# Down projections of six feed-forward stages moved into seven-product units, interleaved with the gate and up units

## What is computed

```
def swiglu(x, w_gate, w_up, w_down):
    return (jax.nn.silu(x @ w_gate) * (x @ w_up)) @ w_down
```

## Time and profile before

| | us |
|---|---|
| median of 3 runs | 3017.22 (3016.87 to 3020.1) |
| the profiled execution, its time | 3015.58 |
| its span in the profile | 3014.3 |
| PE busy | 2961.4 |
| DVE busy | 1835.2 |
| ACT busy | 1348.4 |
| POOL busy | 583.4 |

### The profile page before, as it was taken

One profiled execution on the slowest core, in us unless ns is written; L12 is line 12 of the kernel. 1 busy time (PEld: TensorE's weight loads), 2 busy tenths in 40 slices (PEclk: granted clock), 3 DMA queues, 4 the chain that ended last, 5 costly groups with the idle time before them and its releaser, 6 DMA issues.

```text
span 3014.3 us, 46624 instructions
## 1 busy us (share of the span) xinstructions
PE 2961.4 (98%) x19086; PEld 2616.7 (87%) x19086; DVE 1835.2 (61%) x2832; ACT 1348.4 (45%) x2332; POOL 583.4 (19%) x495
## 2 busy tenths in 40 slices
PE   9999999999999999999999999999999899999999
PEld 7998877899988999886789988899998768788888
DVE  6884566688746887365598853744323866554432
ACT  5552376455524554266455532522223556542321
POOL 0222143302221123034311131100003222200000
PEclk9999999999999999999999999999999999999999
DMA  4333331133332233332223333233233111133332
GB/s 138 113 101 114 97 98 57 57 96 102 115 103 83 92 106 120 93 112 63 64 71 99 106 118 93 78 91 87 90 89 116 50 35 42 36 105 97 93 90 78
DMA packets 76533, 270.10 MB, mean 90 GB/s; under 512 B 8720, under 2 KB 9008, under 8 KB 76064
## 3 DMA queue, kind: packets, MB, share of 16 engines
q1 hardware_dynamic: 74448, 260.08, 28.4%
q0 software_dynamic: 1872, 7.04, 0.7%
HBM read 264.97 MB, written 2.11 MB: 89 GB/s over the span
## 4 chain that ended last, share of the span: by engine, by line
PE 88%; DVE 8%; ACT 2%; issue 1%; DMA 0%; SPq 0%; POOL 0%; DVEq 0%; ACTq 0%
PE psum L424 17%; PE psum L427 17%; PE psum L430 17%; PE psum L677 8%; PE psum L682 8%; PE psum L680 7%; PE psum L488 4%; PE psum L500 2%; PE psum L447 1%; PE psum L443 1%; PE psum L1208 1%; PE psum L445 1%; PE psum L3356 1%; DVE z_sum L1365 1%; DVE w_lo L811 0%
## 5 line engine op out<-in xcount | busy, mean ns | idle before, releaser
L377 DVE TENSOR_TENSOR w_lo<-w_raw,w_hi 128x1024 fp32r<-128x1024 f32 (+1 forms) x300 | 397.2, 1330 | 646.8 <-ACT w_hi L366 646.7
L366 ACT CAST w_hi<-w_raw 128x1024 fp32r<-128x1024 f32 (+1 forms) x346 | 351.4, 1019 | 685.4 <-PE psum L430 643.2
L424 PE MATMUL psum<-x_hi,w_hi 128*128 128x512 f32 (+1 forms) x1648 | 511.2, 351 | 2.6 <-ACT neg_mean L3427 1.8
L427 PE MATMUL psum<-x_hi,w_lo 128*128 128x512 f32 (+1 forms) x1648 | 493.2, 340 | 0.9 <-DVE w_lo L377 0.9
L430 PE MATMUL psum<-x_lo,w_hi 128*128 128x512 f32 (+1 forms) x1648 | 491.2, 339 | 0.1
L424 PEld LDWEIGHTS psum<-x_hi,w_hi 128*128 128x128 f32 x1648 | 283.1, 188 | 58.4 <-issue 18.4
L427 PEld LDWEIGHTS psum<-x_hi,w_lo 128*128 128x128 f32 x1648 | 282.8, 188 | 37.8 <-issue 4.8
L430 PEld LDWEIGHTS psum<-x_lo,w_hi 128*128 128x128 f32 x1648 | 282.8, 189 | 35.9 <-DVE x_lo L3865 0.8
L424 PE MATMUL psum<-h_hi_ffn,w_hi 128*128 128x512 f32 (+1 forms) x792 | 296.4, 374 | 0.0
L430 PE MATMUL psum<-h_lo_ffn,w_hi 128*128 128x512 f32 (+1 forms) x792 | 292.6, 369 | 0.0
L427 PE MATMUL psum<-h_hi_ffn,w_lo 128*128 128x512 f32 (+1 forms) x792 | 292.6, 369 | 0.0
(11 more groups left out here) (436 smaller groups left out, 6760.2 us busy)
## 6 DMA issues: line engine op xcount, KB each, us to landing
w_raw<-in_ffn_gu SPq DMA_DIRECT2D x176, 512.0 KB, 3.6
w_raw<-in_ffn_down SPq DMA_DIRECT2D x64, 512.0 KB, 3.6
w_raw<-in_w_in SPq DMA_DIRECT2D x44, 512.0 KB, 3.6
w_raw<-in_b_gate SPq DMA_DIRECT2D x44, 512.0 KB, 3.6
w_raw<-in_b_up SPq DMA_DIRECT2D x44, 512.0 KB, 3.6
w_raw<-in_b_down SPq DMA_DIRECT2D x32, 512.0 KB, 3.5
w_raw<-in_ffn_down SPq DMA_DIRECT2D x32, 384.0 KB, 3.2
w_raw<-in_b_in SPq DMA_DIRECT2D x24, 512.0 KB, 3.6
```

The costliest lines, as they stand in the source:

```text
L366: nc.scalar.copy(w_hi[s][:, 0:n], w_raw[r][:, 0:n]).then_inc(*w_high.inc(u))
L377: nc.vector.tensor_tensor(w_lo[s][:, 0:n], w_raw[r][:, 0:n], w_hi[s][:, 0:n].bitcast(F32), ALU.subtract).then_inc(*w_low_dve.inc(u))
L424: nc.tensor.matmul(out, w_h, hi[:, c], start=first and i == 0, stop=False)
L427: nc.tensor.matmul(out, w_l, hi[:, c], start=False, stop=False)
```

## The change

- All six FFNs use the combined form, the two of the second block too, with four direct hidden tiles each.
- The first 18 of the 22 contraction tiles of the down projections are taken in three chunks of six (`CHUNKS`). A unit `("d", c, j)` multiplies a chunk with outputs 2j and 2j+1 in seven products of 3 contraction tiles (9 matmuls each); a chunk has four such units. `ffn_units` gives the order: a chunk's units stand among the gate and up units (`"g"`) of the next chunk. A stage has 18 `g` units and 12 `d` units.
- The last four contraction tiles (`TAIL`) are done in direct form at the end, in token halves (16 products of 12 matmuls of 256 columns), with the norm in the manner of `MixNorm` (class `FfnEnd`; `FfnNorm` now derives from `MixNorm`).
- Hidden tiles (class `Hidden`) are held as turned pairs for the first nine pairs (`TURNED`). POOL makes them: `n1`, `t3`, `n2`, `t4` of 256 columns (L630), low parts (L641), and a low part of 4x256 columns (L648) behind one more cast on ACT (`act_turn`). `dve_hidden_low` is gone from DVE.
- A `d` unit adds to `x` in place: POOL first adds each copy `r`, `p1`, `p2` to `x` (`pool_add`, L1199, L1201), then DVE joins (L1114, L1142).
- In `b2_ffn1` POOL applies the late root in the combined form, three more instructions for each hidden tile (`pool_root`).

The core of the diff:

```diff
-COMBINED = {"ffn1_0": 4, "ffn2_0": 4, "ffn1_1": 4, "ffn2_1": 4}
+FIRST_TILES = 4
+COMBINED = {"ffn1_0": 4, "ffn2_0": 4, "ffn1_1": 4, "ffn2_1": 4, "b2_ffn1": 4, "b2_ffn2": 4}
+CHUNKS = ((0, 6), (6, 6), (12, 6))
+TAIL = 18
+TURNED = TAIL // 2
...
+def ffn_units(f0):
+
+    grown = lambda first, end: [("g", f) for f in range(first, end)]
+    down = lambda c, *js: [("d", c, j) for j in js]
+    return (grown(f0, 8) + down(0, 0, 1) + grown(8, 9) + down(0, 2) + grown(9, 10) + down(0, 3)
+            + grown(10, 14) + down(1, 0, 1) + grown(14, 15) + down(1, 2) + grown(15, 16) + down(1, 3)
+            + grown(16, 20) + down(2, 0) + grown(20, 21) + down(2, 1) + grown(21, FT) + down(2, 2, 3))
...
+            def pool_step(self, f):
+
+                for made in self.ready[f]:
+                    pool.wait_ge(*made)
+                if f // 2 < TURNED:
+                    for name in ("t3", "n2", "t4") if f % 2 else ("n1",):
+                        self.pool_combine(name, f // 2)
+                pool.wait_ge(*self.high.at(("h", f)))
+                c, hi, lo = self.of(f)
+                nc.gpsimd.tensor_tensor(lo, self.tile(f)[:, c], hi.bitcast(F32),
+                                        ALU.subtract).then_inc(*self.low.inc(("h", f)))
+
+            def pool_turn(self, pair):
+
+                pool.wait_ge(*self.high.at(("turn", pair)))
+                hi, lo = self.blocks(pair, 3, 4)
+                nc.gpsimd.tensor_tensor(lo, self.raw[:], hi.bitcast(F32),
+                                        ALU.subtract).then_inc(*self.low.inc(("turn", pair)))
...
+                if self.down(i):
+                    even, odd = self.targets(i)
+                    out = {"gate_a": even[:, self.a], "gate_b": even[:, self.b],
+                           "up_b": odd[:, self.b]}[name]
+                    dve.wait_ge(*self.added.at((part, i)))
+                    nc.vector.scalar_tensor_tensor(
+                        out, self.out(b), -self.scale if name == "up_b" else self.scale, snap,
+                        ALU.mult, ALU.add).then_inc(*self.joined.inc((name, i)))
+                    return
...
+            def pool_root(self, name, i):
+
+                tile = self.h.tile(self.units[i][1])
+                c = {"a": self.a, "b": self.b, "again": self.h.columns}[name]
+                if name == "again":
+                    pool.wait_ge(*self.silu.at(self.units[i][1]))
+                else:
+                    pool.wait_ge(*self.joined.at(("gate_" + name, i)))
+                nc.gpsimd.tensor_tensor(tile[:, c], tile[:, c], z_sum[:, c], ALU.mult).then_inc(
+                    *self.rooted.inc((name, i)))
...
+            def pool(self, total):
...
+                for i in range(n + 1):
+                    if i and self.down(i - 1):
+                        self.pool_add("p2", i - 1)
+                    elif i and late:
+                        self.pool_root("b", i - 1)
+                    if i < n and self.down(i):
+                        self.pool_add("r", i)
+                    if i and not self.down(i - 1):
+                        if late:
+                            self.pool_root("again", i - 1)
+                        self.pool_second_half(i - 1)
+                    if i < n:
+                        if self.down(i):
+                            self.pool_add("p1", i)
+                        elif late:
+                            self.pool_root("a", i)
+                    f = self.grown(i - 2)
+                    if f is not None and f % 2 and f // 2 < TURNED:
+                        self.h.pool_turn(f // 2)
+                    f = self.grown(i - 1)
+                    if f is not None:
+                        self.h.pool_step(f)
```

More of the change, by code:

```diff
@@ new lines, in __init__ @@
+                self.t_high, self.t_low = signal("t_high", made), signal("t_low", made)
+                if entry.late:
+                    self.t_scaled = signal("t_scaled", range(HALF_K))
+                for i in units:
+                    raw_read[self.u[i]] = self.summed.at(("s3", i))
+                    raw_read[self.u[i] + 1] = self.low.at(("up", i))
+                    if i in grown:
+                        h.ready[self.units[i][1]] = [self.first_half.at(i), self.second_half.at(i)]
@@ L583, in bank_left, with x_ready @@
+            def x_ready(self, m, i=None):
+                j, odd = divmod(m, 2)
+                c = len(CHUNKS) if i is None else self.units[i][1]
+                if c == 0:
+                    return [self.entry.x_done(m)]
+                last = self.at["d", c - 1, j]
+                if odd:
+                    return [self.joined.at(("up_b", last)), self.first_half.at(last)]
+                return [self.joined.at(("gate_b", last))]
             def bank_left(self, b):
-                fs = range(self.f0, FT)
@@ L720, in block @@
                 s = self.roles[s][0]
-                gate, up = (w_raw[(self.u0 + 2 * f + i) % RAW_SLOTS] for i in range(2))
-                first, second = slice(0, SEQ), slice(SEQ, 2 * SEQ)
+                gate, up = (w_raw[(self.u[i] + j) % RAW_SLOTS] for j in range(2))
+                n = self.half_k(i) * P
                 if name == "later":
-                    pair = lambda tile: tile[:].rearrange("p (a n) -> p a n", a=2)
-                    return squares[:, :, 0:SEQ], pair(w_hi[s]), pair(w_lo[s])
@@ L807, in dve_low @@
[L807 to L818 removed]
+                    if i:
+                        act.wait_ge(*self.joined.at(("gate_a", i - 1)))
@@ new lines, in dve_low, with dve_sum @@
+            def dve_low(self, name, i):
+                raw, hi, lo = self.block(name, i)
+                dve.wait_ge(*self.high.at((name, i)))
+                nc.vector.tensor_tensor(lo, raw, hi.bitcast(F32), ALU.subtract).then_inc(
+                    *self.low.inc((name, i)))
+            def dve_sum(self, name, i):
+                gate, up = (w_raw[(self.u[i] + j) % RAW_SLOTS] for j in range(2))
+                n, u = self.half_k(i) * P, self.u[i]
+                first, second = slice(0, n), slice(n, 2 * n)
+                s1, s2, s4 = (self.sums[s][:, first] for s in ("s1", "s2", "s4"))
@@ L978, in held @@
                 if before:
[L979 to L991 removed]
+                    return [freed(before[-1])]
```

1916 lines of the change are left out of this document (965 added, 951 removed).

## The result

The changed kernel takes 3319.7 us (median of 4 runs, 3318.5 to 3327.6) where the kernel before takes 3017.1 beside it: a ratio of 1.101, with a 95% interval of 1.099 to 1.103. It is slower by 303 us. The forecast was 3151, range 2970 to 3270: right in sign, and outside its range. In short: in the combined parts DVE's round of work, and no longer PE, sets the pace, and POOL's new work both holds up that round and lengthens it. The profiled execution took 3327.6 us with a span of 3326.3.

What follows compares the result with a forecast made beforehand. The prediction took PE to bound the kernel, with a loop without PE hardly shorter. It summed 3015.6 - 108 (PE) + 165 (five stages) + 78 (`b2_ffn1`) = 3151 us, range 2970 to 3270.

Steps and rivals of the forecast that it cites:

- the unit is held by PE, with this loop hardly shorter: Combined unit of the kernel before: PE sets its 10.00 us; the loop through ACT and DVE without PE is hardly shorter.
- PE's share, -108: Matmuls in all stages: -38 for four stages' down projections, -30 for `b2_ffn2`, -40 for `b2_ffn1`; sum -108 us.
- The excess of the five "standard" stages, +33 each: Combined parts of all stages but `b2_ffn1`: DVE and POOL add +33 us a stage, +165 in five.
- turned pairs in runs of gate and up units: Five turned pairs a stage in runs of gate and up units: 2.0 us each uncovered, +10 us.
- hand-overs: p2 behind the step, turned low part, down units' slack: Where down units follow gate and up units: +20.5 us waiting for p2, +9 for low parts, -6.5 from lighter down units.
- POOL's 8.9 us per pair: POOL's work per turned pair: joins cover 2.6 us, DVE idle time 2.5, running ahead 1.3; 2.5 remain.
- `b2_ffn1`, +78: Combined part of `b2_ffn1`: the 33 us of a stage plus 40 and about 5 for late roots on POOL, +78 us.
- `b2_ffn2`, taken as a standard stage: `b2_ffn2` counted among the five stages at +33 us each, with no term for late roots on POOL.
- The stage ends and the rest, 0: End of each stage, DVE's tail beside 23 us of PE: 0, with -3 to +5 us a stage.
- Only the port is shared: Rival: waits are filled and only work sums bind, 276 us against 270 a stage; kernel 2988 us, chance 0.21 with milder forms.
- Waits pile up: Rival: late DVE rounds free raw buffers late, so loads and `s1` wait; +55 a stage, +110 in `b2_ffn1`, 3293 us, chance 0.2.
- The roots alone: Rival: five stages come out even and `b2_ffn1` loses 40 us; kernel near 3015, chance 0.04.

Runs made afterwards that it cites:

- 8: Kernel before, plus four extra 192-column POOL instructions on unused memory behind each hidden tile of its 72 combined units: 3064.5 us, 47 more than the kernel before.
- 5: Changed kernel with most POOL work from hidden tile 10 on, and all roots, cut to 16 columns per instruction (work left out): 3081.5 us.
- 4: Changed kernel with 16 extra PE matmuls, results unused, ahead of the m4 of a down unit behind a turned tile: 3322.5 us.
- 9: Changed kernel with DVE's low part of the last turned block of x moved ahead of the second unit's gate low part: 3323.8 us.
- 10: Changed kernel with ACT copying a down unit's p2 before the hidden tile's cast, where a down unit follows a gate and up unit: 3322.9 us.
- 2: Changed kernel with the late root left out on all but 16 columns of each tile in b2_ffn1 and b2_ffn2: 3248.7 us.
- 11: Changed kernel with four reorderings together: additions on DVE, first two chunks' down units later, last turned block of x early, p2 copy first: 3255.2 us.

## Why the prediction was right in sign and wrong in size

**What bounds the kernel now.** The prediction read "the unit is held by PE, with this loop hardly shorter". DVE's round was 9.96 us in the kernel before (8), as long as PE's unit, and PE can begin such a unit every 9.79 us (5, in the changed kernel). So the loop was full from the start, and in 8 all that stretched it counted in full. What PE alone could do in the kernel before was not run.

**PE's share, -108.** Right as far as it can be seen: where POOL's work was short (5), PE ran the units from `g13` on without a wait, at 116.6 ns a matmul where the term had 119. By that pace PE's own would be 5 us less a stage, and the excesses below as much more.

**The excess of the five "standard" stages, +33 each.** Measured 53.1, 49.4, 51.2 and 49.1 in four of them, +71 us in all against the sum (the fifth, `b2_ffn2`, is below). By the intervals from one unit's first matmul to the next in `ffn2_0`, less PE's own for it (10.0 us between two gate and up units, 8.2 and 9.3 where the two kinds meet, 7.5 between two down units):

| term | forecast | measured |
|---|---|---|
| turned pairs in runs of gate and up units | +10 | 0 by PE's starts (eight units, 9.8 to 10.3 us) |
| hand-overs: p2 behind the step, turned low part, down units' slack | 20.5 + 9 - 6.5 = 23 | 37.4: per chunk 1.9 + 5.8 + 1.3 + 0 + 1.4 + 0 + 5.0 = 15.4 twice, 6.6 in the third |
| first two units | nothing | 7.3 |
| last unit | 0, -3 to +5 | 4.7, of it 1.9 a wait for POOL's total of four tiles |

The seven numbers of a chunk are the excesses of `d00`, `d01`, `g8`, `d02`, `g9`, `d03` and `g10`, and of the same places six tiles on.

So the mechanism of the hand-over was there, and so was its size one wait at a time: what PE waits beyond a step at m7 and m4 of the nine down units sums to 20.4 us in `ffn2_0`, where the sum had 20.5. What failed is the step after it, that these waits are the whole price of a hand-over and that down units give back 6.5. They give back nothing: PE also waits 1.8 us for the turned low part at the first unit of each chunk (row 737.78, 5.5 a stage), and runs at half clock behind four of these waits. Runs 4, 9 and 10 say why adding such items is the wrong book-keeping: they share one bound, DVE's round, and each can be removed or filled without a gain.

**"POOL's 8.9 us per pair": idle time and joins cover all but 2.5.** The idle pieces take up nothing where the round is late (8). And the loss is not where the term had it: PE began the units of a run 9.8 to 10.3 us apart in `ffn2_0` (up to 10.9 in `ffn1_0`). But DVE's rounds in a run did lengthen. In the run `g11` to `g13` of `ffn2_0` the three that begin between 805.6 and 826.2 took 10.79, 9.79 and 10.52 us, and within 0.02 us the same in the run `g17` to `g19`. On average that is 8.17 own, 1.18 stretched and 1.01 idle. DVE is stretched there as much as in 8 (1.10), so POOL's work in a run was not free: DVE lost 0.4 us a unit on PE's 10.0 and PE's starts do not show it. That PE has this much slack only because it comes out of a hand-over late, and that 8, with 18 units in a row and no hand-over, pays at once, is a reading of the traces and was not tried.

**`b2_ffn1`, +78.** Measured 87.9. Of it the roots are 35 or more (2); 45 were taken. Nearly right.

**`b2_ffn2`, taken as a standard stage.** This is the largest single fault, 64 of the 177 us missed: its excess is 96.5 us, not 33. `Mix2Norm`, the norm ahead of it, is a `LateRoot` like that of `b2_ffn1`, so the same three multiplications a tile go to POOL. The diff and the classes showed it; I put the term on one stage only, and at nothing on the other. Run 2 gives the two the same price. The section on the change, ahead of the prediction, names `b2_ffn1` alone too; it holds for both.

**ACT's cast: nothing.** Its second cast cost nothing, as forecast; but ACT's order was in the path at the nine m7 waits (10), if only in name.

**The stage ends and the rest, 0.** 33 us, the remainder of the 312 between the two profiled executions. In it are PE's waits for the norm's sums (L1435, 10 us in nine times) and one of 8.1 us ahead of `b2_ffn1` (L450); the rest I did not follow.

Together: 71 + 10 + 64 + 33 = 178, from 3151 to the profiled 3327.6 but for rounding.

**The signs asked for.** Right: DVE's `gate_b` join on POOL's addition is the largest wait of DVE (126 + 60 us), `b2_ffn1`'s units of gate and up are mostly 12 to 15 us, low parts of 512 columns longer. Wrong: units in a run begin 10.0 us apart and not 11. PE's largest wait is m4 for `up_b` (73.9 us) and not m7 for the copy of p2 (28.7 us in row L1025). PE's idle time is 340 us, where 290 was named. DVE is at 2580 and POOL at 1330, where 2400 and 1160 were named: the contention is mutual, and POOL's 256-column instructions mostly take 0.85 to 1.25 us on average and not 0.74. The text had said it would be wrong in size if the down units and not the pairs held most of the loss; by PE's starts that is what happened (37.4 of 49.4 us in `ffn2_0`).

**The rivals.** "Only the port is shared" took 276 us a stage from volumes. DVE's own time was right (229 measured, 235 taken), the stretched 38 too (41 came out of its sum); what it left out are 52 us of idle time. "Waits pile up" had nearly the size (3293), but by luck: its mechanism did not occur, as DVE's sums waited 3.8 us for loads. What piles up is inside the round. "The roots alone" did not occur either: the standard stages lose 49 us and more.

That the kernel came out slower was not luck: the hand-overs' waits were there. The range failed because its upper end held only more of the same waits. With the 45 us of the roots counted for both stages the forecast would have been 3196 and the range up to 3315, still short by the first and last units, the chunks' first units and the 33 us around.

What stays open: how the 52 us of idle time and 38 stretched in a stage could be lowered together. Every edit that kept the work whole traded one for the other; the best (11) brought the two from 90 to 67 us for 14 us more of own time. The 33 us outside the combined parts are open too.
